# A routed expert stage on one core: router products folded into the projection before it, the deviation kept per token, ranks in five products and overflow counts by an integer shift

## What is computed

```python
x = x + jnp.matmul(merged, w_out[i])
h2 = _rmsnorm(x, ffn_norm[i])              # x * rsqrt(mean(x*x) + eps) * gain
x = x + _hier_moe(h2, ...)

def _hier_moe(h, w_r1, b_r1, w_r2, b_r2, w_gate, w_up, w_down):
    g_logits = jnp.matmul(hf, w_r1) + b_r1                     # 4 groups
    g_sel = jnp.argmax(g_logits, axis=-1)
    p_g = softmax(g_logits) at g_sel
    e_logits = jnp.einsum("nd,gde->nge", hf, w_r2) + b_r2      # 8 experts in each group
    top_v, top_i = lax.top_k(e_sel, 2)
    w_inner = jax.nn.softmax(top_v, axis=-1)
    for e in range(32):
        hid = jax.nn.silu(jnp.matmul(hf, w_gate[e])) * jnp.matmul(hf, w_up[e])
        out = out + comb[:, e:e + 1] * jnp.matmul(hid, w_down[e])
```

## Time and profile before

| what | value |
|---|---|
| median of 3 runs | 2364.31 us (2362.16 to 2365.21) |
| span of the profiled execution | 2358.2 us |
| the three times less that span | 4.0 to 7.0 us |
| mean granted TensorE clock | 0.983 |
| TensorE busy / on the chain that ended last | 96% / 87% |
| VectorE, ScalarE, GpSimd busy | 39%, 33%, 33% |

### The profile page before, as it was taken

The page is one execution under the profiler, slowest core; times in us unless marked ns, Lnnn a source line. Parts: engine busy times, 40 slices in busy tenths (PEclk is TensorE's granted clock), DMA queues, the critical chain, the costliest instruction groups (busy, mean ns, idle before and its releaser), DMA issues.

```text
span 2358.2 us, 30460 instructions
## 1 busy us (share of the span) xinstructions
PE 2261.0 (96%) x12044; PEld 1719.9 (73%) x12044; DVE 919.8 (39%) x1370; ACT 772.5 (33%) x1154; POOL 773.1 (33%) x414
## 2 busy tenths in 40 slices
PE   7999999979999899999999999999999999999997
PEld 5776667633333379668899999888877686888885
DVE  2586453331111463433660362353000524721722
ACT  4335555211111433653421222333322424222222
POOL 3341226211111134204244444334433044544541
PEclk9899999979999999999999999999999999999999
DMA  4421113668999322102223232222322022333330
GB/s 160 144 83 61 45 46 116 245 240 352 353 350 383 115 86 90 45 9 63 65 95 92 89 89 90 90 91 91 96 72 80 1 90 79 98 93 97 98 98 36
DMA packets 69360, 278.03 MB, mean 118 GB/s; under 512 B 13016, under 2 KB 13144, under 8 KB 56960
## 3 DMA queue, kind: packets, MB, share of 16 engines
q1 hardware_dynamic: 59408, 259.61, 31.9%
q0 software_dynamic: 9552, 16.51, 2.0%
q10 hardware_dynamic: 288, 0.34, 0.1%
HBM read 323.58 MB, written 19.42 MB: 145 GB/s over the span
## 4 chain that ended last, share of the span: by engine, by line
PE 87%; DVE 4%; issue 4%; POOL 2%; ACT 2%; DMA 0%; DVEq 0%; POOLq 0%; SPq 0%; ACTq 0%
PE ps L871 19%; PE ps L890 17%; PE ps L1334 7%; PE ps L1093 5%; PE ps L522 4%; PE ps L1136 4%; PE ps L1356 4%; POOL weights_low L2705 2%; PE ps L1295 2%; PE ps L1120 2%; PE ps L641 2%; PE ps L1197 2%; PE ps L732 1%; PE ps L852 1%; PE ps L624 1%
## 5 line engine op out<-in xcount | busy, mean ns | idle before, releaser
L2705 POOL TENSOR_TENSOR weights_low<-weights,parts 128x1024 fp32r<-128x1024 f32 x250 | 632.3, 2534 | 1064.9 <-ACT parts L1884 1064.9
L871 PE MATMUL ps<-parts 128*128 128x264 f32 x2384 | 447.2, 283 | 0.0
L890 PE MATMUL ps<-parts 128*128 128x512 f32 x1344 | 416.1, 390 | 1.3 <-ACT area L1406 1.0
L1884 ACT ACTIVATE parts<-weights 128x1024 fp32r<-128x1024 f32 x257 | 269.1, 1054 | 400.7 <-PE ps L871 133.8
L871 PEld LDWEIGHTS ps<-parts 128*128 128x128 f32 x2384 | 372.9, 188 | 0.0
L871 PE MATMUL ps<-parts,weights_low 128*128 128x264 f32 x1120 | 317.3, 283 | 0.0
L890 PEld LDWEIGHTS ps<-parts 128*128 128x128 f32 x1344 | 252.3, 188 | 56.0 <-issue 1.2
L890 PE MATMUL ps<-parts,weights_low 128*128 128x512 f32 x672 | 262.5, 391 | 0.0
L871 PEld LDWEIGHTS ps<-parts,weights_low 128*128 128x128 f32 x1120 | 211.1, 188 | 0.0
L1334 PE MATMUL ps<-area,normed 128*64 128x512 f32 x752 | 171.5, 597 | 1.6 <-DVE normed L2393 1.6
L2178 DVE TENSOR_TENSOR parts<-normed,parts 128x528 f32 (+1 forms) x64 | 160.5, 2508 | 9.6 <-DVE normed L2177 2.0
(11 more groups left out here) (459 smaller groups left out, 3600.0 us busy)
## 6 DMA issues: line engine op xcount, KB each, us to landing
weights<-in_weights SPq DMA_DIRECT2D x283, 512.0 KB, 3.5
area<-in_experts SPq DMA_DIRECT2D x141, 1024.0 KB
area<-pair_rows SPq DMA_DIRECT2D x4, 1024.0 KB, 7.9
bias_scratch<-bias_vector POOLq DMA_DIRECT2D x1, 2560.0 KB, 18.3
residual<-in_x SPq DMA_DIRECT2D x4, 512.0 KB, 6.4
area<-bias_scratch POOLq DMA_DIRECT2D x1, 2048.0 KB, 9.0
token_rows<-area SPq DMA_DIRECT2D x1, 2048.0 KB, 8.2
out_tiles<-residual SPq DMA_DIRECT2D x4, 512.0 KB, 2.8
```

What stands on the lines that cost most here:

```text
L871: ins = mm(ps[:, b + h, 0:HALF], wt[:, k], x[m * DT + k][:, HALF * h:HALF * h + HALF], start=m == k == j == 0, stop=m == chunks - 1 and k ...
L890: ins = mm(ps[:, b], wt[:, k], x[:, m * DT + k, first:first + SEQ], start=m == k == j == 0, stop=m == chunks - 1 and k == DT - 1 and j == 2)
L1884: fn(high_slot(n, place), RING[:, n % SLOTS], ACT.Copy).then_inc(S["w_hi"], 1)
L2705: g.tensor_tensor(RING_LOW[:, n % SLOTS], RING[:, n % SLOTS], high_slot(n, place), ALU.subtract).then_inc(S["w_lo"], 1)
```

## The change

- ScalarE writes z = x times the norm weight into `HA` behind each projection tile (no deviation in it), and the squares go to another buffer (`ffn_square`, four tiles in turn).
- The router product for tile n-1 is issued on TensorE behind projection tile n; the eighth after the last.
- The squares are summed with one-column products, so that 1/deviation comes out per token on partitions (`ROW_R`, 4 columns). The eight normed tiles are no longer written: the logits are multiplied by `ROW_R` after their transposition, and `HTOK` when it is copied out.
- VectorE copies one half of the logits, ScalarE the other.
- Ranks: four products with a repeated operand of 160, 128, 96 and 64 columns and one of 128 columns.
- Extra windows: (max(count-1, 0)) as a whole number, shifted right by 6.
- The eight small one-hot tables become one instruction of 192 columns.
- The four instructions that end the table of extra windows come behind the index lists.
- `IOTA` lies elsewhere in memory; GpSimd clears the gather buffers only after the last `HTOK` copy.

The core of the diff:

```diff
         SMALL = sb("small", [P, 448])
+        ROW_R = SMALL[:, 0:QT]
         WIDX = area(19456, DT, 8)
...
         DIAGS = area(1472, 2, P)
-        IOTA = area(1728, P)
+        IOTA = area(5888, P)
         SILU = [area(1856, 2 * P), area(2112, 2 * P)]
...
 
+        def ffn_square(n):
+            return area(1024 + 512 * (n % 4), 512)
+
         def merged_high(k):
...
                 begin_stage("dve_evac")
+
+                def route(k):
+                    pe.wait_ge(S["route_z"], k + 1)
+                    at = 64 * (k % 2)
+                    return mm(ps[at:at + 36, 5], WROUT[:, k], HA[:, k], start=k < 2, stop=k >= DT - 2)
+
                 for n in range(DT):
...
                     ins.then_inc(S["tile_done"], 1)
-                begin_stage("dve_evac")
-                rms_sum(HA[:, DT - 1])
-
-                pe.wait_ge(S["wr_in"], w.next("wr_in", 32))
-                for k in range(DT):
-                    pe.wait_ge(S["norm_out"], w.next("norm_out"))
-                    at = 64 * (k % 2)
-                    ins = mm(ps[at:at + 36, 5], WROUT[:, k], HA[:, k], start=k < 2, stop=k >= DT - 2)
-                ins.then_inc(S["route_t"], 1)
-                pe.wait_ge(S["route_c"], 1)
+                    if n == 1:
+                        pe.wait_ge(S["wr_in"], w.next("wr_in", 32))
+                    if n:
+                        route(n - 1)
+                pe.wait_ge(S["sum_part"], w.next("sum_part"))
+                for t in range(QT):
+                    mm(ps[:, 7, t:t + 1], R[:, P * t:P * t + P], ONES[:, 0:1], start=t == 0, stop=True, skip_group_check=True)
+                route(DT - 1).then_inc(S["route_t"], 1)
+                pe.wait_ge(S["norm_sq"], w.next("norm_sq", 8))
+                for t in range(QT):
+                    ins = mm(ps[:, 7, t:t + 1], ffn_square(DT - 1)[:, P * t:P * t + P], ONES[:, 0:1], start=False, stop=True,
+                             skip_group_check=True)
+                ins.then_inc(S["norm_sum"], 1)
+                pe.wait_ge(S["route_c"], 2)
                 for t in range(QT):
...
                 pe.wait_ge(S["route_ev"], w.next("route_ev"))
-                for t in range(QT + 1):
-                    o = ps[:, 6, EXPERTS * t:EXPERTS * t + EXPERTS]
-                    for t2 in range(min(t + 1, QT)):
-                        ins = mm(o, ONES, PICKED[:, t2], start=t2 == 0, stop=t == QT and t2 == QT - 1)
-                    if t < QT:
-                        ins = mm(o, NTRI, PICKED[:, t], start=False, stop=True)
+                rank = ps[:, 6, 0:EXPERTS * (QT + 1)].rearrange("p (t e) -> p t e", e=EXPERTS)
+                for t in range(QT):
+                    mm(rank[:, t:], ONES, PICKED[:, t].unsqueeze(1).to_broadcast([P, QT + 1 - t, EXPERTS]),
+                       start=t == 0, stop=True, skip_group_check=True)
+                ins = mm(rank[:, 0:QT], NTRI, PICKED, start=False, stop=True, skip_group_check=True)
                 ins.then_inc(S["rank_done"], 1)
...
                     act.wait_ge(S["dve_evac"], w.next("dve_evac"))
-                    fn(HA[:, n], XA[:, n], ACT.Square).then_inc(S["norm_sq"], 1)
+                    fn(HA[:, n], XA[:, n], ACT.Copy, scale=vec("ffn_norm", n)).then_inc(S["route_z"], 1)
+                    fn(ffn_square(n), XA[:, n], ACT.Square).then_inc(S["norm_sq"], 1)
                     if 2 <= n < DT - 2:
                         high(last + n + 2, place=IN_WOUT, slots=-1)
-                inverse_deviation(SEQ, D, "eps1")
                 act.wait_ge(S["route_t"], 1)
-                fn(LOGITS_T[0:36], ps[0:36, 5], ACT.Copy)
-                fn(LOGITS_T[64:100], ps[64:100, 5], ACT.Copy).then_inc(S["route_c"], 1)
+                fn(LOGITS_T[0:36], ps[0:36, 5], ACT.Copy).then_inc(S["route_c"], 1)
+                act.wait_ge(S["norm_sum"], w.next("norm_sum"))
+                step(fn(ROW_R, ps[:, 7, 0:QT], ACT.Ln, scale=1.0 / D, bias=vec("eps1")))
+                fn(ROW_R, ROW_R, ACT.Exp, scale=-0.5).then_inc(S["norm_sd"], 1)
                 act.wait_ge(S["route_e"], w.next("route_e"))
                 fn(SMALL[:, 176:192], SMALL[:, 176:192], ACT.Exp).then_inc(S["route_x"], 1)
+                act.wait_ge(S["norm_sd"], 3)
                 for n in range(2 * QT):
-                    evac(HTOK[:, n // 2, 512 * (n % 2):512 * (n % 2) + 512], bank(n))
+                    evac(HTOK[:, n // 2, 512 * (n % 2):512 * (n % 2) + 512], bank(n), scale=ROW_R[:, n // 2:n // 2 + 1])
                 act.wait_ge(S["route_e"], w.next("route_e"))
...
                     accumulate(XA[:, n], ps[:, n % 4], 1.0)
-                    total(n, HA, SEQ, "norm_sq", 8 + 1 + n + 1)
-                dve.wait_ge(S["dve_evac"], w.next("dve_evac", 16 + 16))
-                rms(8, SEQ, "ffn_norm", lambda t: XA[:, t], lambda t: HA[:, t])
+                    if 1 <= n < DT - 1:
+                        dve.wait_ge(S["norm_sq"], 8 + 1 + n + 1)
+                        ins = v.tensor_tensor(R[:, 0:SEQ], ffn_square(0) if n == 1 else R[:, 0:SEQ], ffn_square(n), ALU.add)
+                        if n == DT - 2:
+                            ins.then_inc(S["sum_part"], 1)
+                        else:
+                            step(ins)
+                w.count("dve_evac", 16 + 16)
+                w.count("norm_sum")
                 router()
...
                 step(v.tensor_scalar(FALLING, IOTA[:, 0:8], -1.0, 8.0, ALU.mult, ALU.add))
+                dve.wait_ge(S["wr_in"], w.next("wr_in", 32))
+                dve.wait_ge(S["route_t"], 1)
+                v.tensor_copy(LOGITS_T[64:100], ps[64:100, 5]).then_inc(S["route_c"], 1)
+                dve.wait_ge(S["norm_sd"], w.next("norm_sd"))
                 dve.wait_ge(S["route_done"], w.next("route_done"))
-                dve.wait_ge(S["wr_in"], w.next("wr_in", 32))
-                step(v.tensor_tensor(lt, ps[:, 6, 0:144].rearrange("p (t c) -> p t c", t=4), BR, ALU.add))
-                step(v.tensor_tensor(lt, lt, ps[:, 4, 0:144].rearrange("p (t c) -> p t c", t=4), ALU.add))
+                scaled, rest = small(288, 4, 36), ps[:, 4, 0:144].rearrange("p (t c) -> p t c", t=4)
+                v.tensor_tensor(lt, ps[:, 6, 0:144].rearrange("p (t c) -> p t c", t=4), bc(ROW_R, 4, 36), ALU.mult)
+                step(v.tensor_tensor(scaled, rest, bc(ROW_R, 4, 36), ALU.mult))
+                step(v.tensor_tensor(lt, lt, BR, ALU.add))
+                step(v.tensor_tensor(lt, lt, scaled, ALU.add))
                 g = lt[:, :, 0:4]
...
                 rank = ps[:, 6, 0:128].rearrange("p (t e) -> p t e", t=QT)
+                v.tensor_scalar(one, IOTA[:, 0:EXPERTS], 0.0, 1.0, ALU.mult, ALU.add)
+                step(v.tensor_scalar(base, IOTA[:, 0:EXPERTS], float(WIN), None, ALU.mult))
+                whole = WHERE[:, 0:EXPERTS]
                 dve.wait_ge(S["rank_done"], w.next("rank_done"))
                 step(v.tensor_copy(cnt, ps[:, 6, 128:160]))
-                step(v.tensor_scalar(one, cnt, 0.0, 1.0, ALU.mult, ALU.add))
-                step(v.tensor_scalar(base, IOTA[:, 0:EXPERTS], float(WIN), None, ALU.mult))
-                step(v.tensor_scalar(extra, cnt, float(WIN), None, ALU.is_gt))
-                for m in range(2, SEQ // WIN):
-                    step(v.scalar_tensor_tensor(out=extra, in0=cnt, scalar=float(WIN * m), in1=extra, op0=ALU.is_gt, op1=ALU.add))
+                step(v.tensor_scalar(cnt, cnt, -1.0, 0.0, ALU.add, ALU.max))
+                step(v.tensor_copy(whole, cnt))
+                step(v.tensor_scalar(whole, whole, WIN.bit_length() - 1, None, ALU.logical_shift_right))
+                step(v.tensor_copy(extra, whole))
                 step(v.tensor_tensor_scan(last, one, extra, 0.0, ALU.mult, ALU.add))
...
                 step(v.tensor_copy(ROW_AT, row))
+                v.tensor_tensor(AT_COL, IOTA[:, 0:MOE_PAIRS].unsqueeze(1).to_broadcast([P, TOP_K * QT, MOE_PAIRS]),
+                                bc(COL_AT, TOP_K * QT, MOE_PAIRS), ALU.is_equal)
                 for jt in range(TOP_K * QT):
-                    step(v.tensor_scalar(AT_COL[:, jt], IOTA[:, 0:MOE_PAIRS], COL_AT[:, jt:jt + 1], None, ALU.is_equal))
                     v.tensor_scalar(AT_ROW[:, jt], IOTA, ROW_AT[:, jt:jt + 1], vec("pair_id", jt), ALU.is_equal, ALU.mult)\
...
                 step(v.tensor_scalar(t2, IOTA[:, 0:EXPERTS], float(PARTS_EACH), None, ALU.mult))
-                step(v.tensor_tensor(t2, t2, t1, ALU.mult))
-                step(v.tensor_reduce(COLUMN[:, 0:1], t2, AX, ALU.add))
-                for j in range(2):
-                    ins = v.tensor_scalar(DIAGS[:, j], IDENT, COLUMN[:, j:j + 1], None, ALU.mult)
-                ins.then_inc(S["table_in"], 1)
 
...
                 v.tensor_tensor(FROM, FILLED, held, ALU.add).then_inc(S["rows_known"], 1)
+                step(v.tensor_tensor(t2, t2, t1, ALU.mult))
+                step(v.tensor_reduce(COLUMN[:, 0:1], t2, AX, ALU.add))
+                for j in range(2):
```

(4 more changed lines are left out.)

13 lines of the change are left out of this document (6 added, 7 removed).

## The result

The changed kernel took **2371.81 us** (median of five runs, 2370.53 to 2375.52) where the kernel before, run beside it five times, took 2362.82 us (2362.16 to 2365.21): ratio 1.0037, 95% interval 1.0025 to 1.0049. It is slower by some 9 us, outside the predicted range and on the side that had a chance of 0.13. The profiled execution of the changed kernel took 2374.01 us, its span is 2372.3 us, 14.1 more than the span before (2358.2), at a mean granted clock of 0.977 instead of 0.983.

A forecast was written before the change was run, and what follows sets the result against it. TensorE bounds the kernel, except between the projection's end (E) and the first expert product, where the chain leaves it. A projection 5.8 us longer and that stretch 6.6 shorter sum to -0.8: 2363.5 us, range 2357.5 to 2368.5.

The forecast's parts named there:

- behind it TensorE works without a gap at an unchanged pace: From the first expert product on, TensorE was taken to run unchanged, so every later time only shifts.
- any later stage that changes its length: A listed sign that the prediction is wrong: a stage behind the first expert product becoming longer or shorter.
- Longer projection: Six router products among the projection's products, 0.96 us each, lengthen it by 5.8 us (5.2 to 6.4).
- IOTA at E + 6.9: E is the end of the projection's products; the load VectorE's half of the logits awaits lands 6.9 us later.
- Counts at E + 17.9: After the ranks, the counts come 17.9 us behind the projection's end, instead of 23.6.
- Gather in 5.6 us: The gather before the first expert product falls into three expert loads and lands in 5.6 us (3.4 to 7.8).
- First expert product at E + 37.9: The first expert product starts 37.9 us behind the projection's end instead of 44.4, a gain of 6.6 us.
- The clock's share near the router: Left out of the sum: a shorter half-clock gap ahead of the experts may save or cost up to 1.5 us.
- the products did not hide: Rival: the six router products overlap their neighbours in the projection, so 5.8 us is not paid: 2357.7 us, chance 0.08.
- the gather was not queued behind the loads: Rival: the gather waits 7.8 to 10.7 us behind the expert loads: 2365.8 to 2369.3 us, chance 0.20.
- the first rival: Transfers do not decide: IOTA lands before VectorE needs it or the gather is free of loads: 2357.5 to 2360.5, chance 0.17.
- the rule that the prediction weighed: Transposes do not count as busy for TensorE's clock, so those begun at half clock stay there; sum 0.5 us higher.

The follow-up runs named there:

- after_route_end: The changed kernel with all eight router products issued behind the last projection tile instead of one behind each tile: 2363.49 us, ratio 0.9994.
- after_iota_early: The changed kernel with the IOTA load issued behind the last merge addition, so that VectorE's half of the logits does not wait for it: 2371.00 us, ratio 1.0029.

## Why the prediction was wrong

**The step that failed** is in the first paragraph of the prediction: "behind it TensorE works without a gap at an unchanged pace, and I take every later time as merely shifted". TensorE has gaps in the attention stage at 980 us (3.10 of 4.00 us busy), and the pace changed there: 10.9 of 14.1 us. This was an assumption over 1,860 us of program, and the last row that the prediction names ends at 496 us. It was listed as what would make the prediction wrong ("any later stage that changes its length"), but had no price in the range. Neither the router nor the transfers had part in it: fillers or 14 idle copies in the changed kernel bring it back to ratio 0.9996 and 1.0000.

Without the fall, the forecast of no measurable change would have held: 2363.06 us with the copies against the 2363.5 on record, though 1.1 us above the kernel before beside it and not 0.8 below. Point by point:

- **Longer projection, +5.8 (5.2 to 6.4): mis-sized, 7.38.** A lone product of 36 columns takes 0.98 on the chain, as forecast (0.96), but the tile behind it gets longer too. From one of them to the next it is 6.66 us (417.40 to 424.06), where the 24 products of a tile start 0.227 apart in the trace of before, 5.44 a tile: 1.22 for each lone product, 7.3 for six. The bounds priced the product alone, not what it does to its neighbour. Seven of them in a bunch cost 0.52 each (`after_route_end`).
- **IOTA at E + 6.9: right, E + 6.6** (5.61 us in flight, 5.9). The logits were copied at E + 7.6 (7.8). Turning them took 1.93 us instead of 1.1, at a clock of 0.50, so VectorE's first instruction came at E + 9.6 (9.1).
- **Copies of token rows to E + 16.3: right, E + 16.2.**
- **Counts at E + 17.9: E + 19.0.** The chain shows why: one instruction of VectorE on 128x4 numbers (line 2356) lasts 1.39 us, its neighbours 0.18. GpSimd clears the gather buffers beside it, which the diff moved to this place and for which the prediction has no term:

```profile
473.60 1.84 POOL L2655 MEMSET area<- 128x1024 f32 x2 [14.66 <-ACT area L1418]
474.09 1.38 DVE L2356 TENSOR_SCALAR small<-small 128x4 f32<-128x4 f32 x1
```

  The clears end at 475.44, the instruction 0.03 later. In all nine kernels that hold the change it ends 0.02 to 0.03 us behind the end of one of the two clears: of the second in four (1.38 to 1.44 long), of the first in five (0.49 to 0.55). In the kernel before the clears come at 450.48, ahead of VectorE's first instruction of this part (453.19). So it very likely waits for GpSimd, but no run clears the buffers at another time to test it. The later points follow 1.1 late: scan at E + 20.1 (19.0), and the gather is issued at E + 30.8 (29.4).
- **Gather in 5.6 us (3.4 to 7.8): 4.21.** Landed at E + 35.0, the very number forecast, by luck: it is issued 1.4 us late and takes 1.4 less.
- **First expert product at E + 37.9: E + 37.84**, by the same luck.
- **Sum -0.8: +0.8**, all from the mis-sized products.
- **The clock's share near the router, up to 1.5 us:** of the 1.87 us by which the first expert product is late, 1.3 have come back by 980 us; no run tells what gave them. The clock that mattered was another.

Of the rivals, the transfers did decide (VectorE waited for IOTA to E + 6.6), the products did not hide (0.08), and the gather was not queued behind the loads in this kernel (4.21 us, below its turning point of 6.4); it was in `after_iota_early`, where it took most of what the first rival hoped for from an early IOTA. The transposes give a second reading on the rule that the prediction weighed (the Trainium skill, TensorE: Matmul & The Clock Gate, section Part 4: PE-mode transpose). A stretch of the changed kernel, columns as above:

```profile
466.00:468.00 2.00, 2.00 (x16) 1.93 (x15) 0.91 (x4) 0.00 (x0) 0.00 (x0) 0.50 1.02 416
468.00:470.00 2.00, 2.00 (x11) 2.00 (x10) 1.76 (x9) 1.33 (x4) 0.00 (x0) 0.50 1.03 410
470.00:472.00 2.00, 2.00 (x17) 2.00 (x16) 1.69 (x11) 2.00 (x5) 0.00 (x0) 0.83 1.02 408
```

From 464.97 to 466.90 us TensorE turns the logits, with ordinary products; from there to 472.2 it runs nothing but the transposes of the token rows (line 678), and after nearly four us of them, near 470.7, the granted clock goes to 1.00. By the rule it would have stayed at 0.50, so this trace speaks against it again.

## What to carry to other kernels

When a change takes or adds instructions on one engine, look through the rest of the program for stages where TensorE and that engine wait for each other in turn, with gaps in TensorE's work at full clock (3.10 of 4.00 us busy here): a pause of a fifth of a microsecond there can cost ten, and with 14 products of no use put into TensorE's waits none of the 24 runs shows the long time. Before a later stage is called merely shifted, read its clock before and after; and before a change is judged by such a loss, pad the engine's stream back to its old place and time it again. And a transfer that the chain waits for, as the gather here, belongs ahead of the large loads in the order of issue: 3.52 us when the loads came 1.5 us behind it, 8.66 when they came 0.3 us ahead of it.

## What was not expected of the hardware

- The place of an engine's instructions in its stream is worth time: packets of 8192 bytes bring it during the run, and where one block ends VectorE pauses 0.17 us between a reduction and its readout, or 0.04 at a place some instructions away (997.68 to 998.09 in the kernel before, against 0.37 elsewhere). Both readouts come 0.41 us behind the start of their reduction, of 0.31 us in the first case and of 0.44 in the second, as if the longer one hid most of the pause. Fourteen instructions more took 8.8 us out of the changed kernel, and 114 put 11.8 into the kernel before.
- A fall of TensorE's granted clock in a stage where it and VectorE wait for each other lasted 20.5 to 23.9 us in the four profiles that show it, though no idle time of TensorE was longer than 0.8 us in the stage ahead of it in the changed kernel. VectorE then waits longer for each block of logits, as the products run at half pace (0.94 us at 1005.27 in the changed kernel, nothing at the same place before).
- One product of 36 columns in full precision costs 1.2 us alone among single-pass products and 0.52 in a bunch of seven of its kind.
- A VectorE instruction on 128x4 numbers took 0.49 to 1.44 us beside GpSimd's clears and ended with one of them each time, where its neighbours took 0.18.
